# Two-layer decoder trunk on eight cores: the first value weights loaded in halves, token factors by bf16 rows, the last head slot undivided

## The chip, the cores and the metric

The kernel runs as one launch on the 8 cores of one Trainium2 chip. The metric is device time of the slowest core, in microseconds (us). Each core owns 1024 of the 8192 tokens and computes everything for them, with a halo of 2688 earlier tokens whose keys and values it works out again for itself. A core has TensorE (PE in the profile: matmuls, and PEld: its weight loads), VectorE (DVE), ScalarE (ACT), GpSimd (POOL) and SyncE (SP); here POOL and SP mostly issue DMA transfers.

## What is computed

Cut to the parts that matter here, the reference is:

```python
def _rms_norm(x, g):
    xf = x.astype(jnp.float32)
    y = xf * lax.rsqrt(jnp.mean(xf * xf, axis=-1, keepdims=True) + NORM_EPS)
    return (y * g.astype(jnp.float32)).astype(x.dtype)

def _dilated_attention_mixer(h, positions, w_in):     # layer 0
    q, k, v, q_mem = jnp.split(h @ w_in, [ATTN_W, 2 * ATTN_W, 3 * ATTN_W], axis=-1)
    q = _partial_rotary(q.reshape(b, s, ATTN_HEADS, HEAD_DIM), positions)
    k = _partial_rotary(k.reshape(b, s, ATTN_HEADS, HEAD_DIM), positions)
    ...
    for g, (window, dilation) in enumerate(((128, 1), (512, 4), (2048, 16))):
        o, l = _dilated_group(q[:, :, sl], k[:, :, sl], v[:, :, sl], window, dilation)
    ...                       # merged per head slot by the softmax denominators

for i in range(2):
    h = _rms_norm(x, mix_norm[i])
    mix_out, q_mem = mixer(h)   # layer 0: dilated attention, layer 1: spatial gating
    mem_out = _memory_attention(q_mem, _rms_norm(mem, mem_norm[i]), w_mem_kv[i])
    x = x + jnp.concatenate([mix_out, mem_out], axis=-1) @ w_out
    x = x + _swiglu(_rms_norm(x, ffn_norm[i]), w_gate[i], w_up[i], w_down[i])
return _rms_norm(x, final_norm)
```

D_MODEL is 2048, a head has 128 columns, and each of the three groups has four head slots.

## The kernel before

**Order.** All work on the five engines is recorded as operations with the regions they read and write. A list scheduler (`Prog.schedule`) then walks them by its own cost estimates and fixes the order on each engine; on the chip each engine runs its list strictly from front to back and waits by semaphores. So an operation that waits holds up everything behind it on its engine. A changed cost, cover or dependency can reorder the lists of all engines.

**The first stage.** It runs from 0 to about 345 us and makes the keys and values of the halo. The halo comes in blocks: 0 to 3 (512 tokens each, group with dilation 16), 4 (512, dilation 4) and 5 (128, dilation 1); the own tokens are two blocks of 512 (own 0, own 1, tile `hT`), and after them come the memory tokens. `norm_T` treats one block. Its `front` loads x transposed in four quarters of 0.5 MB on POOL's queue (into `stg_54` or `stg_55`, or `hT` for own blocks), squares each quarter on ACT (L592), adds two squares on DVE (L601), and sums over the features with four matmuls against ones (L603; block 0 skips the add, L597). The sum lies in PSUM bank 6 or 7, by turns from block to block. ACT turns it into the norm factor by Ln (L606) and Exp (L607), laid out along a row. For the raw blocks 0 to 4 the x tiles are only multiplied by the gain (L623, DVE); the norm factor is multiplied in later. The key path has it in its rotary tables (L693) and in L537. The value path needs it as a column per 128 tokens: four one-row fp32 matmuls (L610) turn the row into columns in the same bank, and DVE copies them out (L612). Own blocks are scaled on DVE at once (L621).

**The units.** `vunit` (L662) makes the values of 128 tokens with 16 matmuls of 512 columns into one of the banks 0 to 5, and ACT evicts them with the column factor (L671). `kunit` (L684) makes the keys of one head, 16 matmuls, and DVE applies the rotary (`rotary`: L537, L540, L541, L543, L545). `own_v` (L718) and `qk_units` (L766) do the same for own tokens. Weights come in 1 MB pieces into four ring slots (`Ring.load`, L455): two for the values of a group, two for its keys. In the listing here V0, K0, V1, K1 and so on are the units of block 0, 1 and so on. At the very start 24 matmuls on a constant (L811) run between the first sums.

**The attention.** `attend(s)` treats head slot s. Its last part (L1000 to L1009) takes the reciprocal of the softmax denominators (in banks 6 and 7) and multiplies the sums (banks 4 and 5) into `attnT`. For slots 0 to 2 that is one Ln (L1002) and one Exp (L1003) on ACT over 1024 columns and one multiply on DVE. For slot 3 it is divided in halves: Ln and Exp on ACT for the first 512 columns, a reciprocal on DVE (L1000) for the other 512, then two multiplies on DVE. After it the output projection begins (L1133).

Of the kernel before, what the change touches and what calls it, by code (L numbers as in the profile page):

```python
# [298 lines left out]
def build():  # L299
# [140 lines left out]
    class Ring:  # L440
# [5 lines left out]
        def load(self, src, half=False, at=None):  # L446
# [39 lines left out]
    one = small[112:113]  # L486
    dve(lambda v: v.memset(one, 1.0), [], [kreg("one")], 1)
# [64 lines left out]
    def norm_T(src_of, n, g0, keep_rs=None, own=None, raw=False):  # L552
# [22 lines left out]
        def front(after=(), pre=True):  # L575
            dmas = []
            for qd in range(4):
                dst = quarter(qd)
                if not pre and qd == 1:
# [69 lines left out]
    def halo_units(bi, nrm):  # L649
# [6 lines left out]
        def vunit(tt):  # L656
            def f():
                ws = [weights(("v", gi, h), w0[W0_V[gi][h]]) for h in range(2)]
                b = nextbank(P0B)
                for k0 in range(0, 16, 2):  # L660
# [1165 lines left out]
```

The softmax here doesn't subtract the row's maximum and nothing guards it: scores larger than these inputs give would overflow.

## Time and profile before

| | us |
|---|---|
| time, median of 3 runs | 2610.54 |
| lowest, highest run | 2609.48, 2611.22 |
| the profiled execution's own time | 2610.54 |
| its span on the slowest core, core 0 | 2608.9 |
| spans of the other cores | 2591.3 to 2606.8 |
| PE busy in the span | 2533.4 (97%) |
| DVE busy in the span | 1390.0 (53%) |
| ACT busy in the span | 712.7 (27%) |

Some 1.6 us of the time lie outside the span. All the rows below are of core 0. The start of a stage or a wait is in us from the span's start. A row of the timeline gives start, length, engine, line and operation, written tile and read tiles, and in brackets how long the engine had been idle before it and what ended that. Where the engine named had long been done, a DMA ended it.

### The profile page before, as it was taken

Reading aid. Unit: us, or ns where it says so; the run is one execution under the profiler, and the core shown is the slowest. Engines: PE = TensorE matmul, PEld = TensorE weight load, DVE = VectorE, ACT = ScalarE, POOL = GpSimd, SP = SyncE. Lnnn points to the kernel's source line nnn. Section 1 sums busy time; section 2 is a strip of 40 time slices with the busy share of each in tenths; the row PEclk is TensorE's granted clock in tenths of the full one; section 3 lists DMA queues with packets and bytes.
Section 4 is the critical chain, followed back from the end, with each engine's and each line's share of the span. In section 5 each row is a group of like instructions: output and inputs, shape, how many; then the busy total and the mean of one; then the engine's idle time right before and its main releaser. Section 6 shows DMA issues by size and latency. Waiting matters only on the chain.

```text
span 2608.9 us, 34534 instructions; the slowest of 8 cores (2591.3 to 2608.9 us)
## 1 busy us (share of the span) xinstructions
PE 2533.4 (97%) x12775; PEld 1191.2 (46%) x12775; DVE 1390.0 (53%) x2359; ACT 712.7 (27%) x1121; POOL 145.2 (6%) x247
## 2 busy tenths in 40 slices
PE   7999999999999999999999999999999999999997
PEld 3454445544444444444444444444444444444443
DVE  4862638867444443456667234237444444467666
ACT  3622134344222322210004431034222332210004
POOL 2100000000000000000000000000000000000002
PEclk9999999999999999999999999999999999999999
DMA  9845654345656656557644634334666656667554
GB/s 158 132 72 98 118 109 72 60 146 99 121 108 121 116 103 113 106 129 142 139 114 82 134 65 81 67 63 86 115 111 119 114 105 111 110 135 158 117 127 145
DMA packets 91893, 288.45 MB, mean 111 GB/s; under 512 B 6736, under 2 KB 56528, under 8 KB 68304
## 3 DMA queue, kind: packets, MB, share of 16 engines
q0 software_dynamic: 36912, 218.00, 48.7%
q1 hardware_dynamic: 54816, 68.24, 8.0%
q8 instruction: 104, 1.70, 0.3%
q14 instruction: 61, 0.50, 0.1%
HBM read 471.70 MB, written 32.51 MB: 193 GB/s over the span
## 4 chain that ended last, share of the span: by engine, by line
PE 89%; DMA 4%; DVE 4%; issue 2%; ACT 1%; POOL 0%; DVEq 0%; ACTq 0%; POOLq 0%; SPq 0%
PE psall L1243 39%; PE psall L1395 17%; PE psall L766 6%; PE psall L1634 4%; PE psall L1542 3%; PE psall L1591 3%; PE psall L684 3%; PE psall L662 2%; PE psall L718 2%; PE psall L1133 2%; DMA hid<-fs_74 1%; PE psall L1606 1%; PE psall L786 1%; PE psall L1098 1%; DMA stg_54<-xT 1%
## 5 line engine op out<-in xcount | busy, mean ns | idle before, releaser
L1034 DVE TENSOR_TENSOR xs<-psall,xs 128x512 f32<-128x512 f32 x400 | 270.2, 688 | 244.7 <-PE psall L1395 161.5
L1243 PE MATMUL psall<-hTq,ft_71 128*128 128x512 f16 x704 | 166.3, 379 | 0.6 <-DVE hTq L1123 0.6
L1243 PE MATMUL psall<-hTq,ft_72 128*128 128x512 f16 x704 | 166.3, 379 | 0.0
L1243 PEld LDWEIGHTS psall<-hTq,ft_71 128*128 128x128 f16 x704 | 68.7, 98 | 83.5 <-issue 0.9
L1243 PEld LDWEIGHTS psall<-hTq,ft_72 128*128 128x128 f16 x704 | 68.8, 98 | 82.6
L1243 PE MATMUL psall<-hTq,fr_67 128*128 128x512 f16 x384 | 87.3, 379 | 1.0 <-DVE hTq L1104 1.0
L1040 ACT ACTIVATE junkB_129<-xs 128x1024 bf16<-128x1024 f32 x16 | 16.8, 1052 | 248.2 <-DVE xs L1034 247.6
L1243 PE MATMUL psall<-Sq_65,ft_72 128*128 128x512 f16 (+2 forms) x368 | 83.5, 370 | 0.0
L1243 PE MATMUL psall<-Sq_65,ft_71 128*128 128x512 f16 (+2 forms) x368 | 83.5, 370 | 0.0
L1243 PE MATMUL psall<-Sq_64,ft_72 128*128 128x512 f16 x352 | 83.2, 379 | 0.0
L1243 PE MATMUL psall<-Sq_64,ft_71 128*128 128x512 f16 x352 | 83.2, 379 | 0.0
L1243 PE MATMUL psall<-hTq,fr_70 128*128 128x512 f16 x352 | 79.9, 379 | 0.0
L1243 PE MATMUL psall<-hTq,fr_69 128*128 128x512 f16 x352 | 79.7, 379 | 0.0
L1243 PE MATMUL psall<-hTq,fr_68 128*128 128x512 f16 x320 | 72.7, 379 | 0.0
L1040 ACT ACTIVATE junkB_128<-xs 128x1024 bf16<-128x1024 f32 x8 | 8.5, 1057 | 233.3 <-DVE xs L1034 232.8
L1222 DVE TENSOR_TENSOR ft_71<-fr_67 128x2048 f16<-128x2048 f16 x22 | 26.9, 1225 | 82.5 <-PE psall L1243 81.8
L1222 DVE TENSOR_TENSOR ft_72<-fr_70 128x2048 f16<-128x2048 f16 x20 | 24.5, 1225 | 84.8 <-PE psall L1243 84.8
L1222 DVE TENSOR_TENSOR ft_71<-fr_69 128x2048 f16<-128x2048 f16 x20 | 24.5, 1225 | 83.1 <-PE psall L1243 83.1
L1222 DVE TENSOR_TENSOR ft_72<-fr_68 128x2048 f16<-128x2048 f16 x20 | 24.5, 1224 | 80.0 <-PE psall L1243 79.4
L1104 DVE TENSOR_TENSOR hTq<-psall,gT_s 128x1024 f16<-128x1024 f16 x48 | 56.9, 1218 | 17.7 <-PE psall L1098 17.2
L1249 ACT COPY snap_79<-psall 128x512 f32<-128x512 f32 x59 | 34.5, 585 | 113.5 <-PE psall L1243 113.5
L1249 ACT COPY snap_77<-psall 128x512 f32<-128x512 f32 x58 | 34.0, 585 | 115.1 <-PE psall L1243 115.1
(1341 smaller groups left out, 4726.4 us busy)
## 6 DMA issues: line engine op xcount, KB each, us to landing
fr_67<-wgu POOLq DMA_DIRECT2D x24, 1024.0 KB, 9.5
fr_69<-wgu POOLq DMA_DIRECT2D x22, 1024.0 KB, 9.8
fr_70<-wgu POOLq DMA_DIRECT2D x22, 1024.0 KB, 9.1
fr_68<-wgu POOLq DMA_DIRECT2D x20, 1024.0 KB, 9.5
ring_0_137<-w POOLq DMA_DIRECT2D x8, 1024.0 KB, 9.2
xs<-xo SPq DMA_DIRECT2D x8, 1024.0 KB, 10.2
y<-xs SPq DMA_DIRECT2D x16, 512.0 KB, 4.1
ring_0_138<-w POOLq DMA_DIRECT2D x7, 1024.0 KB, 10.5
```

The lines of the kernel that those rows point to most:

```text
L662: pe([(lambda t, k=k, w=w: t.matmul(bank(b), hb[k * n + tt * 128:k * n + tt * 128 + 128], w[(k % 8) * 512:(k % 8 + 1) * 512], start=(k == ...
L684: pe([(lambda t, k=k: t.matmul(bank(b)[:, 0:n], w[k * 256 + c0:k * 256 + c0 + 128], hb[k * n:(k + 1) * n], start=(k == 0), stop=(k == 15)) ...
L766: proj(b, 512, [(lambda t, k=k: t.matmul(bank(b), w[k * 256 + c * 128:k * 256 + c * 128 + 128], hT[k * TOK + th * 512:k * TOK + th * 512 + ...
L1034: dve(lambda v: v.tensor_tensor(out=xa, in0=bank(b), in1=xa, op=ALU.add), [PB(b), xr], [xr], 512)
L1104: dve(lambda v, b=b, gb=gb, dst=dst: v.tensor_tensor(out=dst, in0=bankb(b).rearrange("p (a c) -> p a c", c=128), in1=gb, op=ALU.mult), [PB ...
L1222: dve(lambda v: v.tensor_tensor(out=T[0:2048], in0=w[1024:3072], in1=w[0:2048], op=ALU.subtract), [w.r(0, 3072)], [T.r(0, 2048)], 2048, 2)
L1243: pe([(lambda t, k=k: t.matmul(bank(b)[:, lo:lo + n], W[blk * 1024 + k * 128:blk * 1024 + k * 128 + 128], f(k)[:, lo:lo + n], start=(first ...
L1249: act(lambda a: a.copy(out=s_.ap, in_=bank(b)), [PB(b)], [s_.r()], 512)
L1395: pe([(lambda t, k=k: t.matmul(bank(b), f(u, k), w[k * 512:(k + 1) * 512], start=(first and k == 0), stop=(last and k == hG - 1), skip_gro ...
L1542: pe([(lambda t_, k=k, b=b, hf=hf, ws=ws, t=t: t_.matmul(bank(b), hTq[hq_(hf * 8 + k, t * 128, 128)], ws[hf][k * 512:(k + 1) * 512], start ...
L1591: proj(b, 512, [(lambda t, k=k, b=b, c=c, th=th, w=w: t.matmul(bank(b), w[k * 256 + c * 128:k * 256 + c * 128 + 128], hTq[hq_(k, th * 512, ...
L1634: pe([(lambda t_, k=k, hh=hh, hf=hf: t_.matmul(bank(b), gTm[(hh * 8 + k) * TOK + t * 128:(hh * 8 + k) * TOK + t * 128 + 128], ws[hh][k * 5 ...
```

## The change

Four things change, all in the first stage and in the last head slot.

1. **Halves.** The two 1 MB pieces of the first value weights are loaded in halves of 0.5 MB. On POOL's queue each half stands behind one quarter of block 0's x. A value matmul waits for the half that it reads, no longer for the whole piece. The load of the position table (`tki`) waits for the first half in place of the constants. 16 matmuls on a constant remain of 24.
2. **Token factors.** ACT casts the row of norm factors to bf16 (hi), DVE subtracts it from the fp32 row (lo, bf16), and eight bf16 matmuls of one column each, hi and lo for four token tiles, sum both into columns. They are recorded not in `front` but by the block's second value unit, and the evictions of the first two value units are recorded behind them.
3. **Banks.** Keys of block 5 and the memory units of layer 0 take banks 0 to 5 in place of 2 to 5.
4. **Last head slot.** It is treated as slots 0 to 2 are, undivided.

```diff
+    rhl = [sb(f"rhl{i}", 196 * KB + 1024 * i, 1024) for i in range(2)]
...
+                for i in range(2):
+                    sl = slice(i * 2048, (i + 1) * 2048)
+                    parts.append(lambda sl=sl, i=i: pooldma(lambda g: g.dma_start(out=rb[sl], in_=src[:, sl]), [], [rb.r(sl.start, sl.stop)],
+                                                            f"w{at}{'b' * i}", 1.05))
...
                 dmas.append(pooldma(lambda g, dst=dst, qd=qd: g.dma_start(out=dst, in_=src_of(qd)), [],
                                     qreg(qd), f"x{sid}_{qd}", 4 * n * 512 / 1e6, after=after))
+                if between is not None:
+                    between[qd]()
...
+            def cols():
+                col = small[104 + 4 * sid:104 + 4 * sid + n // 128]
+                hi, lo = rhl
+                act(lambda a: a.copy(out=hi[0:n][0:1], in_=rb[0:n][0:1]), [rb.r(0, n)], [hi.r(0, n)], n)
+                dve(lambda v: v.tensor_tensor(out=lo[0:n][0:1], in0=rb[0:n][0:1], in1=hi[0:n][0:1], op=ALU.subtract),
+                    [rb.r(0, n), hi.r(0, n)], [lo.r(0, n)], n, lat=3)
+                pe([(lambda t, tt=tt, i=i: t.matmul(bank(b)[:, tt:tt + 1], rhl[i][tt * 128:(tt + 1) * 128][0:1], ones[0:1, 0:1],
+                                                    start=(i == 0), stop=(i == 1)))
+                    for tt in range(n // 128) for i in range(2)], [hi.r(0, n), lo.r(0, n), ON_R], [PB(b)], 1)
+                dve(lambda v: v.tensor_copy(out=col, in_=bank(b)[:, 0:n // 128]), [PB(b)], [kreg(f"col{sid}")], 4)
             if raw:
-                col = small[104 + 4 * sid:104 + 4 * sid + n // 128]
-                pe([(lambda t, tt=tt: t.matmul(bank(b)[:, tt:tt + 1], rb[tt * 128:(tt + 1) * 128][0:1], one[0:1], start=True, stop=True))
-                    for tt in range(n // 128)], [rb.r(0, n), kreg("one")], [PB(b)], 128)
-                dve(lambda v: v.tensor_copy(out=col, in_=bank(b)[:, 0:n // 128]), [PB(b)], [kreg(f"col{sid}")], 4)
+                cols_.append(cols)
...
-                       [w.r()] + [hb.r(k * n + tt * 128, k * n + tt * 128 + 128) for k in (k0, k0 + 1)], [PB(b)], 512)
+                       [w.r(k0 % 8 * 512, (k0 % 8 + 2) * 512)] + [hb.r(k * n + tt * 128, k * n + tt * 128 + 128) for k in (k0, k0 + 1)], [PB(b)], 512)
...
-                    act(lambda a: a.activation(out=dst, in_=src, func=AF.Copy, scale=rs), [PB(b), kreg(f"col{sid}")],
-                        Vh.r3(4, HALO, tile * 128, tile * 128 + 128), 512)
+                    nrm[4].append(lambda: act(lambda a: a.activation(out=dst, in_=src, func=AF.Copy, scale=rs), [PB(b), kreg(f"col{sid}")],
+                                              Vh.r3(4, HALO, tile * 128, tile * 128 + 128), 512))
+                    if tt:
+                        for f in nrm[4]:
+                            f()
+                        nrm[4].clear()
                     return
...
-                b = nextbank(P0B if raw else (2, 3, 4, 5))
+                b = nextbank(P0B)
...
+        act(lambda a: a.activation(out=rden.ap, in_=denA, func=AF.Ln), [PB(6), PB(7)], [rden.r()], 1024, tbl="exp")
+        act(lambda a: a.activation(out=rden.ap, in_=rden.ap, func=AF.Exp, scale=-1.0), [rden.r()], [rden.r()], 1024, tbl="exp")
...
-            if h == 1:
-                dve(lambda v, rd=rd: v.reciprocal(rd, bank(7)), db, [rr], n)
...
+        dve(lambda v: v.tensor_tensor(out=row.rearrange("p (m r) -> p m r", r=16), in0=by_tok(accA), in1=by_tok(rden.ap), op=ALU.mult),
+            [PB(4), PB(5), rden.r()], [attnT.r(s * TOK, (s + 1) * TOK)], 1024)
```

The new lines shift the numbers in the changed kernel: the sums are L607 and L613, the value units L680, the key units L706, the columns L625, the constant matmuls L835, the squares L602, Ln and Exp L616 and L617.

TensorE, from the end of block 0's sums, before: sums of x (L597) with matmuls on a constant (L811), the columns (L610), then V0 from ring slots 137 and 138 and K0 from 139.

```order
L811 MATMUL psall<-cmat_s 128x512 x5
L597 MATMUL psall<-sq_51,cmat_s 128x512 x4
L811 MATMUL psall<-cmat_s 128x512 x2
L610 MATMUL psall<-small,rsr_125 128x1 x4
L662 MATMUL psall<-ring_0_137,stg_54 128x512 x32
L662 MATMUL psall<-ring_0_138,stg_54 128x512 x32
L684 MATMUL psall<-stg_54,ring_0_139 128x512 x32
```

TensorE, from its first operation, after: V0 (L680) reads ring slots 139 and 140, which now name the first value weights; `stg_54` is block 0's x.

```order
L680 MATMUL psall<-ring_0_139,stg_54 128x512 x4
L607 MATMUL psall<-sq_51,cmat_s 128x512 x4
L680 MATMUL psall<-ring_0_139,stg_54 128x512 x12
L835 MATMUL psall<-cmat_s 128x512 x4
L607 MATMUL psall<-sq_52,cmat_s 128x512 x4
L835 MATMUL psall<-cmat_s 128x512
L680 MATMUL psall<-ring_0_139,stg_54 128x512 x16
L835 MATMUL psall<-cmat_s 128x512 x4
L607 MATMUL psall<-sq_53,cmat_s 128x512 x4
L835 MATMUL psall<-cmat_s 128x512
L680 MATMUL psall<-ring_0_140,stg_54 128x512 x16
L835 MATMUL psall<-cmat_s 128x512 x4
```

V0 has moved in between the sums of block 0, a quarter's worth at a time.

TensorE around own 0's first sum, before: L603 on `sq_52` is the second sum of block 2, L603 on `sq_51` the first sum of own 0; L684 is K1 and L662 with `stg_54` V2.

```order
L603 MATMUL psall<-sq_52,cmat_s 128x512 x4
L684 MATMUL psall<-stg_55,ring_0_139 128x512 x8
L684 MATMUL psall<-stg_55,ring_0_140 128x512 x8
L610 MATMUL psall<-small,rsr_125 128x1 x4
L684 MATMUL psall<-stg_55,ring_0_140 128x512 x8
L662 MATMUL psall<-ring_0_137,stg_54 128x512 x2
L603 MATMUL psall<-sq_51,cmat_s 128x512 x4
L684 MATMUL psall<-stg_55,ring_0_140 128x512 x8
L662 MATMUL psall<-ring_0_137,stg_54 128x512 x12
L662 MATMUL psall<-ring_0_138,stg_54 128x512 x2
L603 MATMUL psall<-sq_53,cmat_s 128x512 x4
```

The same place after: the first L613 is the second sum of block 2, the next the first sum of own 0; then come tiles of V2 (L680).

```order
L613 MATMUL psall<-sq_52,cmat_s 128x512 x4
L613 MATMUL psall<-sq_51,cmat_s 128x512 x4
L680 MATMUL psall<-ring_0_139,stg_54 128x512 x8
L680 MATMUL psall<-ring_0_140,stg_54 128x512 x8
L680 MATMUL psall<-ring_0_139,stg_54 128x512 x6
L613 MATMUL psall<-sq_53,cmat_s 128x512 x4
L680 MATMUL psall<-ring_0_139,stg_54 128x512 x2
L680 MATMUL psall<-ring_0_140,stg_54 128x512 x2
```

Own 0's first sum now follows block 2's second sum directly, and 32 matmuls of V2 stand ahead of the second half of K1 (`ring_0_142`), which stood ahead of nearly all of V2.

ScalarE at the same place, after: L602 on `hT` are the squares of own 0, L616 and L617 are Ln and Exp, on `rsr_125` for block 2 and on `rsb_123` for own 0.

```order
L602 ACTIVATE sq_51<-hT 128x2048
L616 ACTIVATE rsr_125<-psall,small 128x512
L602 ACTIVATE sq_52<-hT 128x2048
L617 ACTIVATE rsr_125<-rsr_125 128x512
L602 ACTIVATE sq_53<-hT 128x2048
L602 ACTIVATE sq_51<-hT 128x2048
L616 ACTIVATE rsb_123<-psall,small 128x512
L617 ACTIVATE rsb_123<-rsb_123 128x512
L622 CAST rhl_127<-rsr_125 1x512
L689 ACTIVATE Vh<-psall,small 128x4x128 x4
```

Block 2's Ln stands between own 0's first and second square, and the evictions of V1 (L689) stand behind own 0's Exp and block 2's cast.

ScalarE around block 3's norm, after: L602 on `stg_55` are its squares, L602 on `hT` those of own 1, `rsr_126` is block 3's factor.

```order
L602 ACTIVATE sq_51<-stg_55 128x2048
L602 ACTIVATE sq_52<-stg_55 128x2048
L602 ACTIVATE sq_53<-hT 128x2048
L616 ACTIVATE rsr_126<-psall,small 128x512
L617 ACTIVATE rsr_126<-rsr_126 128x512
L602 ACTIVATE sq_51<-hT 128x2048
L689 ACTIVATE Vh<-psall,small 128x4x128 x3
L602 ACTIVATE sq_52<-hT 128x2048
L689 ACTIVATE Vh<-psall,small 128x4x128
L622 CAST rhl_127<-rsr_126 1x512
```

ScalarE at that place, before, where the same Ln and Exp are L606 and L607.

```order
L592 ACTIVATE sq_51<-stg_55 128x2048
L671 ACTIVATE Vh<-psall,small 128x4x128 x2
L592 ACTIVATE sq_53<-hT 128x2048
L592 ACTIVATE sq_52<-stg_55 128x2048
L592 ACTIVATE sq_52<-hT 128x2048
L606 ACTIVATE rsr_126<-psall,small 128x512
L592 ACTIVATE sq_51<-hT 128x2048
L607 ACTIVATE rsr_126<-rsr_126 128x512
L592 ACTIVATE sq_53<-hT 128x2048
```

In both, squares of own 1 stand ahead of block 3's Ln; on TensorE the columns of block 2 (L625), which share bank 6 with block 3's sum, now stand behind that Ln:

```order
L706 MATMUL psall<-stg_54,ring_0_141 128x512 x24
L613 MATMUL psall<-sq_52,cmat_s 128x512 x4
L706 MATMUL psall<-stg_54,ring_0_141 128x512 x8
L613 MATMUL psall<-sq_51,cmat_s 128x512 x4
L625 MATMUL psall<-cmat_s,rhl_127 128x1
L625 MATMUL psall<-cmat_s,rhl_128 128x1
```

Before, block 2's columns (L610 in the fence of TensorE above) were made ahead of V2.

## Rows read from the trace of the kernel before

**Rows 1.** The page's list of busy time: TensorE, weight loads and the other engines.

```profile
PE 2533.4 (97%) x12775; PEld 1191.2 (46%) x12775; DVE 1390.0 (53%) x2359; ACT 712.7 (27%) x1121; POOL 145.2 (6%) x247
```

**Rows 2.** Timeline of the opening on TensorE: columns, V0's second half, K0, V1.

```profile
28.12 1.02 PE L610 MATMUL psall<-small,rsr_125 1*128 1x1 f32 x8 [1.32 <-ACT rsr_125 L607]
...
37.73 7.07 PE L662 MATMUL psall<-ring_0_138,stg_54 128*128 128x512 bf16 x32
...
44.64 7.07 PE L684 MATMUL psall<-stg_54,ring_0_139 128*128 128x512 bf16 x32
...
58.45 2.75 PE L662 MATMUL psall<-ring_0_137,stg_55 128*128 128x512 bf16 x12
```

**Rows 3.** Timeline of POOL's queue: when two ring pieces are issued.

```profile
5.39 0.59 POOL L455 DMA_DIRECT2D ring_0_138<-w  x1
5.91 0.60 POOL L455 DMA_DIRECT2D ring_0_139<-w  x1
```

**Rows 4.** DMA issues, 0 to 110 us: times, size of one, us to landing.

```profile
ring_0_138<-w POOLq DMA_DIRECT2D x1, 1024.0 KB, 29.9
ring_0_139<-w POOLq DMA_DIRECT2D x1, 1024.0 KB, 35.4
```

**Rows 5.** Timeline, 58 to 94 us: an add, a square, an Ln, K1's end.

```profile
58.44 1.20 DVE L601 TENSOR_TENSOR sq_52<-sq_52,sq_53 128x2048 bf16<-128x2048 bf16 x1
...
82.18 1.91 ACT L592 ACTIVATE sq_51<-hT 128x2048 bf16<-128x2048 bf16 x1
...
83.98 0.69 ACT L606 ACTIVATE rsr_125<-psall,small 128x512 f32<-128x512 f32 x1
...
91.27 1.89 PE L684 MATMUL psall<-stg_55,ring_0_140 128*128 128x512 bf16 x8
```

**Rows 6.** Timeline of POOL's queue: loads of block 3 (second pair), then own 1.

```profile
93.70 1.07 POOL L582 DMA_DIRECT2D stg_55<-xT  x2 [1.92 <-PE psall L684]
94.74 3.01 POOL L582 DMA_DIRECT2D hT<-xT  x4
```

**Rows 7.** DMA issues near 94 us: size of one, us to landing.

```profile
stg_55<-xT POOLq DMA_DIRECT2D x2, 512.0 KB, 12.7
...
hT<-xT POOLq DMA_DIRECT2D x1, 512.0 KB, 16.8
```

**Rows 8.** Waits of TensorE, 95 to 600 us: us in total, times, longest.

```profile
PE psall L1133 <- DVE attnT L1009: 5.8, 1, 5.8
...
PE psall L718 <- DVE hT L621: 1.6, 1, 1.6
PE psall L603 <- DVE sq_52 L601: 1.5, 1, 1.5
```

**Rows 9.** Stretches: length, busy us by engine, granted clock (PEclk), DMA share, GB/s.

```profile
198.00:199.00 1.00, 1.00 (x6) 0.55 (x5) 0.02 (x1) 0.88 (x2) 0.00 (x0) 1.00 1.02 213
...
300.00:301.00 1.00, 1.00 (x4) 0.30 (x2) 0.00 (x0) 0.00 (x0) 0.00 (x0) 0.50 0.95 164
...
545.00:554.00 9.00, 5.25 (x13) 1.61 (x14) 5.34 (x7) 1.87 (x4) 0.00 (x0) 0.50 0.70 210
```

**Rows 10.** Timeline: a ring slot's load, and the matmul that waited for it.

```profile
287.57 0.53 POOL L455 DMA_DIRECT2D ring_0_138<-w  x1 [8.11 <-PE psall L662]
...
297.78 0.59 PE L766 MATMUL psall<-hT,ring_0_138 128*128 128x512 bf16 x2 [3.72 <-DVE t_1_118 L540]
```

**Rows 11.** Timeline of the end of slot 0 (undivided), then of slot 3 (halves).

```profile
415.98 1.03 ACT L1002 ACTIVATE rden_121<-psall 128x1024 f32<-128x1024 f32 x1
...
418.28 1.89 DVE L1009 TENSOR_TENSOR attnT<-psall,rden_121 128x1024 bf16<-128x1024 f32 x1
...
542.84 0.60 ACT L1002 ACTIVATE rden_121<-psall 128x512 f32<-128x512 f32 x1 [3.10 <-PE psall L951]
...
548.59 0.58 PE L1133 MATMUL psall<-ring_0_139,attnT 128*128 128x512 bf16 x1 [5.85 <-DVE attnT L1009]
```

**Rows 12.** Instructions of one line, 402 to 404 us: ns, min/median/max.

```profile
L928 PE MATMUL psall<-QK_47,KTh x9: 193/193/219, 402.2 to 403.1; 128*128 128x64 bf16 x8, 128*128 128x128 bf16 x1
```

More of the change, by code:

```diff
@@ L444, in build, with load @@
         gen = {}
-        def load(self, src, half=False, at=None):
+        def load(self, src, half=False, at=None, parts=None):
             if at is None:
@@ L485, in build @@
     dve(lambda v: v.memset(eps_ap, EPS), [], [kreg("eps")], 1)
-    one = small[112:113]
-    dve(lambda v: v.memset(one, 1.0), [], [kreg("one")], 1)
     act(lambda a: a.activation(out=small[254:255], in_=eps_ap, func=AF.Ln), [kreg("eps")], [kreg("warm")], 1, tbl="exp")
@@ L573, in qreg, with front @@
             return [sg.r(k * step + base, k * step + base + n) for k in range(qd * 4, qd * 4 + 4)]
-        def front(after=(), pre=True):
+        cols_ = []
+        def front(after=(), pre=True, between=None):
             dmas = []
@@ L629, in scale @@
             return f
-        return front, [scale(k) for k in range(16)], sg, (rb, sid)
+        return front, [scale(k) for k in range(16)], sg, (rb, sid), cols_
     def x_src(bi):
@@ L732, in f @@
                 w = weights(("mk", layer, m // 2), wkv[layer * 4 + m // 2])
-                b = nextbank((0, 1) if layer else (2, 3, 4, 5))
+                b = nextbank((0, 1) if layer else P0B)
                 c0 = (m % 2) * 128
@@ L744, in f @@
                 ws = [weights(("mv", layer, h), wkv[layer * 4 + 2 + h]) for h in range(2)]
-                b = nextbank((0, 1) if layer else (2, 3, 4, 5))
+                b = nextbank((0, 1) if layer else P0B)
                 for hf in range(2):
@@ L800, in build @@
     n0 = xnorm(0)
-    n0[0](pre=False)
-    weights(("v", 2, 0), w0[W0_V[2][0]])
-    weights(("v", 2, 1), w0[W0_V[2][1]])
-    spdma(lambda q: q.dma_start(out=tki.ap, in_=posr), [kreg("cm")], [tki.r()], "c5", 0.5)
+    v0p = []
+    for h in range(2):
+        rb = R.load(w0[W0_V[2][h]], parts=v0p)
+        held["v", 2, h] = (rb, R.gen[rb.off // KB])
+    n0[0](pre=False, between=v0p)
+    spdma(lambda q: q.dma_start(out=tki.ap, in_=posr), [held["v", 2, 0][0].r(0, 2048)], [tki.r()], "c5", 0.5)
     for h in range(2):
@@ L811, in build @@
     warm = [P.op("pe", lambda t: t.matmul(bank(WB).rearrange("p (a b) -> p a b", b=128), ones, M_own.unsqueeze(1).to_broadcast([128, 4, 128]), start=True, stop=True), [ON_R, OW_R], [], 0.43, prio=1e9)
-            for _ in range(24)]
+            for _ in range(16)]
     n1 = xnorm(1)
@@ L991, in attend @@
         state["prev"]()
+        act(lambda a: a.activation(out=rden.ap, in_=denA, func=AF.Ln), [PB(6), PB(7)], [rden.r()], 1024, tbl="exp")
+        act(lambda a: a.activation(out=rden.ap, in_=rden.ap, func=AF.Exp, scale=-1.0), [rden.r()], [rden.r()], 1024, tbl="exp")
         row = attnT[s * TOK:(s + 1) * TOK]
-        for h in range(2) if s == 3 else (None,):
-            sl, hs = (slice(0, TOK), slice(0, 16)) if h is None else (slice(h * 512, h * 512 + 512), slice(h * 8, h * 8 + 8))
-            n, nr = sl.stop - sl.start, hs.stop - hs.start
-            rd, rr = rden[sl], rden.r(sl.start, sl.stop)
-            ab, db = ([PB(4), PB(5)], [PB(6), PB(7)]) if h is None else ([PB(4 + h)], [PB(6 + h)])
-            if h == 1:
-                dve(lambda v, rd=rd: v.reciprocal(rd, bank(7)), db, [rr], n)
-            else:
-                act(lambda a, rd=rd, sl=sl: a.activation(out=rd, in_=denA[:, sl], func=AF.Ln), db, [rr], n, tbl="exp")
-                act(lambda a, rd=rd: a.activation(out=rd, in_=rd, func=AF.Exp, scale=-1.0), [rr], [rr], n, tbl="exp")
-        for h in (1, 0) if s == 3 else (None,):
-            sl, hs = (slice(0, TOK), slice(0, 16)) if h is None else (slice(h * 512, h * 512 + 512), slice(h * 8, h * 8 + 8))
-            n, nr = sl.stop - sl.start, hs.stop - hs.start
-            by_tok = lambda a, nr=nr: a.rearrange("p (r m) -> p m r", r=nr)
-            out = row.rearrange("p (m r) -> p m r", r=16)[:, :, hs]
-            dve(lambda v, out=out, sl=sl, by_tok=by_tok: v.tensor_tensor(out=out, in0=by_tok(accA[:, sl]), in1=by_tok(rden[sl]), op=ALU.mult),
-                ([PB(4), PB(5)] if h is None else [PB(4 + h)]) + [rden.r(sl.start, sl.stop)], [attnT.r(s * TOK, (s + 1) * TOK)], n)
+        by_tok = lambda a: a.rearrange("p (r m) -> p m r", r=16)
+        dve(lambda v: v.tensor_tensor(out=row.rearrange("p (m r) -> p m r", r=16), in0=by_tok(accA), in1=by_tok(rden.ap), op=ALU.mult),
+            [PB(4), PB(5), rden.r()], [attnT.r(s * TOK, (s + 1) * TOK)], 1024)
     def x_load(t, after=()):
```

4 lines of the change are left out of this document (3 added, 1 removed).

## The prediction

> **What bounds the kernel now.** I read the busy times first. TensorE works 97% of the span and no other engine is above 53% [rows 1]; so time is won only where TensorE waits, runs at its lower clock, or does work that can go. All edits lie in the first stage (to 345 us) and at the end of head slot 3 (543 us), and from there the program is the same; a microsecond won or lost is passed on to the end. I then read where TensorE waits there: the opening until K0 starts at 44.64 [rows 2], one wait of 1.6 and two of 1.5 (the second of them not shown), one of 5.8 at slot 3's end [rows 8], and one of 3.72 [rows 10]. The granted clock came third: behind the 1.5 us wait at 197.5 it stays at 1.00 (2.4 GHz), behind those of 3.7 and 5.8 us it is 0.50 (1.2 GHz) for a while [rows 9]. At the upper level matmuls of 512 columns lie (44.64 - 37.73) / 32 = 0.216 us apart [rows 2]. The sum is made against the profiled execution, 2610.54 us, 1.6 of it outside the span; it is also the median.
>
> **The opening.** Before, V0 begins after the last x quarter's norm and ends at 44.64; after, V0 follows the x quarters and the weight halves. The total up to the second weight piece is unchanged, so its last half lands where that piece did: 5.39 + 29.9 = 35.3 [rows 3, 4]. Behind it are 16 matmuls, 3.5 us, and the columns: TensorE is through at 39. But K0 needs the next piece, which lands at 5.91 + 35.4 = 41.3, in the same place of the queue as before. So K0 starts at 41.4 in place of 44.64: **-3.2**. That is the cap of this edit, not V0's 15 us. The eight constant matmuls that go stood in waits for DMA and are worth nothing.
>
> **The columns.** Before, four fp32 matmuls are eight passes, 1.02 us [rows 2], five times (one row stands for them). After, eight one-column bf16 matmuls. The nearest row has nine small bf16 ones start between 402.2 and 403.1, with other work among them [rows 12]: eight take 0.8 at most and nothing at least; I take 0.27, because other matmuls filled most of that stretch. That saves 0.75 each time, between 0.2 and 1.0: **-3.75** in all, where nobody waits for them. The cast and the subtraction (a row of 512, priced like an Ln, 0.69 [rows 5]) lie beside TensorE's work.
>
> **First new wait: own 0's first sum.** K0 takes 58.45 - 44.64 = 13.8 [rows 2] and ends at 55.2; 112 matmuls, sums among them, reach to the end of block 2's second sum, 112 x 0.216 = 24.2: 79.4. Before, 26 matmuls and the columns, 6.6 us, stood between that sum and own 0's first one. After, the two follow directly, and the order of ScalarE puts block 2's Ln ahead of own 0's second square. So the chain from sum to sum lies open: Ln 0.69, square 1.91, add 1.20 [rows 5], 0.2 for hand-overs: **+4.0**, within 0.3 either way, to 83.4. It hangs on no transfer, and an earlier or later arrival does not change it. Queued behind the waiting sum on TensorE stand V2's tiles.
>
> **Small waits up to K1's end.** Own 0's second sum waits for its last quarter's square and add (0.6), block 1's columns for own 0's Ln, which shares bank 7 (0.2), K1's second half for V1's evictions, which now stand behind Exp and cast (0.5): **+1.3**, from nothing to 2.5.
>
> **Second new wait: block 3's norm.** K1's second half now stands behind 32 matmuls of V2. Before, K1 ends at 91.27 + 1.89 = 93.2 [rows 5]. After: 83.4 + own 0's two sums 1.7 + 32 of V2 6.9 + the small waits 1.3 + 32 of K1 6.9 = 100.2, 7 us later (6.4 at the reads that POOL waits for). POOL's loads of block 3 and own 1 wait for K1's reads of `stg_55` [rows 6], and move by 6.4. Before, block 3's last quarter lands at about 94.2 + 12.7 = 107 and own 1's first at 94.74 + 16.8 = 111.5 [rows 6, 7]; after, at 113.4 and 118. TensorE arrives at block 3's second sum behind 64 more matmuls and a sum, 14.7, at 114.9; square and add [rows 5] are done at 116.6 (1.7 lost). Block 2's columns behind it share bank 6 with that sum and wait for its Ln, and ScalarE holds that Ln behind own 1's first square, which ends at 118 + 1.9 = 119.9: the columns come at 120.6 (3.0 lost). V3's first matmuls then wait for the first K2 head's rotary (2.2, its chain on DVE), and 0.5 is spread: **+7.4**. Bounds: 3 if the transfers land 4 us sooner in a quiet queue, 9 if DVE is behind. The 1.6 us wait before own 0's values [rows 8] is then covered: **-1.6**.
>
> **Clock.** Work at 0.50 costs half its busy time: 5.25 us of it behind the 5.85 us wait, 2.6 [rows 9]; behind the 3.72 us wait some 3.3 us ran at it (one of them shown), 1.6. The new waits are 4.0 and, with little work between, 1.7 + 3.0 + 2.2. I take 1.6 and 2.1: **+3.7**; nothing to 5.2. The Trainium skill (TensorE: Matmul & The Clock Gate, HAM oscillation — how this bites in real kernels) advises finishing a product's K tiles before waiting for DMA, lest the clock fall in each wait. That speaks against V0 by quarters. The trace agrees for a wait of 3.72, not for one of 1.5 [rows 9].
>
> **A ring slot later.** Block 5's values free a slot for query weights, which came 297.7 - 287.57 = 10.1 us after their issue, 3.72 of them waited for [rows 10]. In the new order that read stands one query piece of eight matmuls later against what covers the load: **+1.7**, from nothing to 2.7 if the clock falls further.
>
> **Last head slot.** Before, 548.59 - 542.84 = 5.75 [rows 11]. Undivided as in slot 0, from Ln's start to the multiply's end: 418.28 + 1.89 - 415.98 = 4.2, and a hand-over of 0.1 [rows 11]. **-1.5**. The wait is still longer than 3.72, so its slow stretch stays. Banks 0 to 5 for block 5's keys and the memory, and the dropped memset, cost nothing: their units lie behind queries that TensorE has ready.
>
> **Sum.** -3.2 - 3.75 + 4.0 + 1.3 + 7.4 - 1.6 + 3.7 + 1.7 - 1.5 = +8.05: 2610.5 + 8.0 = **2618.5**. With the low terms (no small waits, second wait 3, no clock, no slot) it is -3.1, 2607.4; with the high ones (2.5, 9, 5.2, 2.7) +13.4, 2623.9.
>
> **Rivals.**
>
> *The opening at half clock.* V0 now runs in bursts between landings; if the level is 0.50 there, the 16 matmuls behind the last half take 16 x 0.43 = 6.9, the columns are through at 42.5, the gain falls to 2.0, and K0's first eight matmuls pay 1.7: 2618.5 + 1.2 + 1.7 = 2621.4. This is what that section of the Trainium skill (TensorE: Matmul & The Clock Gate) would make of it. For it: behind the wait of 3.72 us it fell to 0.50 [rows 9]. Against it: at 198 us, behind a wait of 1.5, it is 1.00 [rows 9], and the bursts leave waits of about that length: a megabyte lands in 41.3 - 35.3 = 6 us, and 25 matmuls of a quarter fill 5.4 of them. That the halves don't do what they say (the last quarter's square or scale holds V0 up) ends at the same time. Chance 0.15.
>
> *The lag is absorbed* (not slower). Downstream lie waits of 1.5, 1.5 and 3.72 [rows 8, 10]. If what ends them does not move with TensorE, because it hangs on transfers issued early, they swallow up to 5 of the lag: 2613.5; if the clock also holds through the broken second wait, 2611.4. It decides once these waits shrink to under 0.5. Against it: those loads are issued when TensorE frees a buffer, as the one of 287.57 was. Chance 0.28.
>
> *The loads win* (faster). If block 3's and own 1's transfers land 5 us sooner, the second wait is at most 2, the small waits go and the clock holds: -3.2 - 3.75 + 4.0 + 2.0 - 1.6 - 1.5 = -4.05; with one wait of 1.5 downstream covered 2605, and with columns that save 1.0 each 2603.7. For it: only eight transfers stand in that queue. Against it: so it was before, and the last took 12.7 and 16.8 [rows 7]. Chance 0.17.
>
> **How the numbers follow.** Forecast 0.40, half clock 0.15, absorbed 0.28, loads win 0.17. About 0.2% (5.2 us) is what a measurement of this kernel tells from no change. So slower 0.55, same 0.28, faster 0.17. The range takes in the absorbed case, most of the faster one (2603) and the high bound with the half clock's 1.2 on it: 2603 to 2626. The likeliest case alone spans 2615 to 2625.
>
> **What would show it.** Right: K0 at 41 to 42; TensorE idle for about 4 us before own 0's first sum near 80 us; block 3's POOL issues at 96 to 101; three waits between 114 and 124; a granted clock of 0.50 behind them; the last slot's wait at 4.3. Wrong: a sum of own 0 that follows block 2's without a gap, K1 ending before 95, or a clock of 1.00 from 80 to 130 us.

## The result: slower, by the two waits and what they drag along

| | before | after |
|---|---|---|
| time, median of 4 runs, us | 2610.88 | 2625.22 |
| ratio to before, 95% interval | | 1.0051 [1.0031, 1.0070] |
| profiled execution's own time | 2610.54 | 2621.14 |
| its span on the slowest core | 2608.9 (core 0) | 2619.5 (core 2) |
| TensorE busy in the span | 2533.4 | 2527.6 |

The changed kernel is slower by 0.51%, some 13 us, though TensorE is busy 6 us less. The ratios here and below leave out executions in which some cores were disturbed; without the one such execution of the changed kernel (2902 us) its median is 2624.2. The profiled execution is the shortest of the changed kernel's, 10.6 us above that of before, and the readings below explain that one.

Waits of TensorE from 30 to 600 us, after (us in total, times, longest). They answer to [rows 8].

```profile
PE psall L613 <- DVE sq_51 L611: 7.8, 2, 4.1
PE psall L788 <- DMA ring_0_140<-w: 5.5, 1, 5.5
PE psall L1144 <- DVE attnT L1020: 4.8, 1, 4.8
PE psall L613 <- DVE sq_53 L611: 3.0, 1, 3.0
PE psall L680 <- DVE t_0_119 L547: 2.9, 2, 2.6
PE psall L706 <- DMA ring_0_141<-w: 1.7, 1, 1.7
PE psall L613 <- DVE sq_52 L611: 1.7, 2, 1.1
PE psall L625 <- ACT rsr_126 L616: 1.2, 1, 1.2
```

The wait of 1.6 before own values is gone. New are two waits for squares of a norm (7.8 in two), one for columns (1.2) and one for a rotary (2.6); longer are those for the query weights (5.5, before 3.7) and for the memory's norm (3.0, before 1.5). In the timeline of TensorE the new ones stand here:

```profile
41.15 6.85 PE L706 MATMUL psall<-stg_54,ring_0_141 128*128 128x512 bf16 x31 [1.74 <-DMA ring_0_141<-w]
...
78.94 1.02 PE L613 MATMUL psall<-sq_52,cmat_s 128*128 128x512 bf16 x4
84.01 1.17 PE L613 MATMUL psall<-sq_51,cmat_s 128*128 128x512 bf16 x4 [4.05 <-DVE sq_51 L611]
...
95.31 7.07 PE L706 MATMUL psall<-stg_55,ring_0_142 128*128 128x512 bf16 x31
...
120.80 1.02 PE L613 MATMUL psall<-sq_51,cmat_s 128*128 128x512 bf16 x4 [3.75 <-DVE sq_51 L611]
123.01 0.16 PE L625 MATMUL psall<-cmat_s,rhl_127 1*128 1x1 bf16 x1 [1.19 <-ACT rsr_126 L616]
...
125.95 1.01 PE L680 MATMUL psall<-ring_0_139,stg_55 128*128 128x512 bf16 x2 [2.59 <-DVE t_0_119 L547]
```

K0 starts at 41.15, before at 44.64 [rows 2]. The sum at 78.94 is block 2's second, that at 84.01 own 0's first. ScalarE shows what lies between them: block 2's Ln, then own 0's second square.

```profile
80.06 0.69 ACT L616 ACTIVATE rsr_125<-psall,small 128x512 f32<-128x512 f32 x1 [0.79 <-PE psall L613]
80.64 1.90 ACT L602 ACTIVATE sq_52<-hT 128x2048 bf16<-128x2048 bf16 x1
...
117.41 1.91 ACT L602 ACTIVATE sq_52<-stg_55 128x2048 bf16<-128x2048 bf16 x1 [1.50 <-DMA stg_55<-xT]
120.38 1.91 ACT L602 ACTIVATE sq_53<-hT 128x2048 bf16<-128x2048 bf16 x1 [1.06 <-DMA hT<-xT]
122.20 0.67 ACT L616 ACTIVATE rsr_126<-psall,small 128x512 f32<-128x512 f32 x1
```

The second group belongs to the waits near 120. The 3.75 us of the sum at 120.80 are a wait for block 3's last quarter: its square starts at 117.41, when its transfer has landed. Own 1's first square, which also waited for its transfer, stands ahead of block 3's Ln; that adds only some 0.4 us to the 1.19 of the columns, since the sum ends at 121.82 and the Ln starts at 122.20. POOL issued block 3's loads at 90.69 and 93.70 [rows 6] before, at 99.47 and 102.91 after:

```profile
90.69 1.09 POOL L582 DMA_DIRECT2D stg_55<-xT  x2 [27.33 <-PE psall L684]
```

```profile
99.47 1.08 POOL L590 DMA_DIRECT2D stg_55<-xT  x2 [39.93 <-PE psall L706]
102.91 1.05 POOL L590 DMA_DIRECT2D stg_55<-xT  x2 [2.36 <-PE psall L706]
```

Granted clock, after (columns as in [rows 9]): in the opening, behind the two waits, behind the memory's norm, and at the last head slot.

```profile
15.00:30.00 15.00, 14.77 (x58) 5.97 (x57) 2.28 (x8) 3.82 (x2) 0.00 (x0) 1.00 1.04 188
...
86.00:88.00 2.00, 2.00 (x7) 0.63 (x5) 1.97 (x5) 1.44 (x1) 0.00 (x0) 0.50 0.00 1
...
126.00:128.00 2.00, 2.00 (x5) 0.64 (x6) 1.94 (x3) 2.00 (x4) 0.00 (x0) 0.50 1.16 193
...
267.00:269.00 2.00, 2.00 (x6) 0.65 (x5) 0.00 (x0) 0.58 (x1) 0.00 (x0) 0.50 0.57 119
...
560.00:565.00 5.00, 5.00 (x18) 1.96 (x17) 2.10 (x4) 1.87 (x4) 0.00 (x0) 0.74 0.92 272
```

Behind the waits of 4.05, of 7.5 in three and of 2.96 us the level is 1.2 GHz for a while; the row of 267 is new, behind the memory's wait. That wait, before and after:

```profile
256.64 0.60 PE L603 MATMUL psall<-sq_53,cmat_s 128*128 128x256 bf16 x4 [1.51 <-DVE sq_53 L601]
```

```profile
264.34 0.60 PE L613 MATMUL psall<-sq_53,cmat_s 128*128 128x256 bf16 x4 [2.96 <-DVE sq_53 L611]
```

It is not the same on every core: on the other seven of the changed kernel's profiled execution it is between 0 and 1.7 us.

How far the changed kernel lies behind, at the same operation in both:

| operation | before | after | behind |
|---|---|---|---|
| K0 starts | 44.64 | 41.15 | -3.5 |
| own values start | 141.17 | 149.09 | 7.9 |
| first sum of the memory's norm | 256.64 | 264.34 | 7.7 |
| queries behind the ring load | 297.78 | 310.67 | 12.9 |
| output projection starts | 548.59 | 559.74 | 11.2 |
| end of the span | 2608.9 | 2619.5 | 10.6 |

All of it is lost before 311 us, and a little given back at the last head slot. The 7.7 of the memory's row is too small by 1.7: in the changed kernel one piece of eight matmuls of own values stands behind that sum which stood ahead of it before.

### The profile page after: what moved, and what is told of

It is laid out like the page before. It is cut to its first block, busy times and chain, and to the rows that moved or that the text cites. A ratio compares the mean times of both kernels' runs of the same rounds, so it can differ in the third digit from the quotient of the medians.

```text
span 2619.5 us, 34458 instructions; the slowest of 8 cores (2601.2 to 2619.5 us)
## 1 busy us (share of the span) xinstructions
PE 2527.6 (96%) x12688; PEld 1188.4 (45%) x12767; DVE 1388.7 (53%) x2361; ACT 717.1 (27%) x1126; POOL 146.1 (6%) x249
## 4 chain that ended last, share of the span: by engine, by line
PE 87%; DMA 6%; DVE 4%; issue 3%; ACT 1%; POOL 0%; DVEq 0%; ACTq 0%; POOLq 0%; SPq 0%
PE psall L1254 39%; PE psall L1406 18%; PE psall L788 6%; PE psall L1645 4%; PE psall L1602 3%; PE psall L740 2%; PE psall L1553 2%; DMA stg_55<-xT 2%; PE psall L1144 2%; PE psall L680 2%; PE psall L706 1%; PE psall L808 1%; DMA ring_0_215<-wkv 1%; DMA hid<-fs_74 1%; PE psall L1109 1%
```

## The experiments

Two theories stood at first. D: recording the columns late (the deferral) costs. H: the halves cost, because V0's early start reorders everything behind it.

**e1: the deferral undone.**

```diff
-                cols_.append(cols)
+                cols()
...
-                    nrm[4].append(lambda: act(lambda a: a.activation(out=dst, in_=src, func=AF.Copy, scale=rs), [PB(b), kreg(f"col{sid}")],
-                                              Vh.r3(4, HALO, tile * 128, tile * 128 + 128), 512))
-                    if tt:
...
+                    act(lambda a: a.activation(out=dst, in_=src, func=AF.Copy, scale=rs), [PB(b), kreg(f"col{sid}")],
+                        Vh.r3(4, HALO, tile * 128, tile * 128 + 128), 512)
```

> The changed kernel with one thing undone: the columns of token factors are recorded in the block's own norm again (still cast, subtract and eight bf16 matmuls), and each value eviction right behind its unit. Theory D (the deferral costs): recorded by the second value unit, a block's columns stand behind the next norm that uses the same PSUM bank, and so the value evictions, their banks and the second half of K1 wait for that norm. Without it the 4.1 us wait before own 0's first sum and the three waits between 116 and 126 us (7.5) go, the loads of block 3 are issued at 88 to 94 us, and the time falls by 8 to 13 us from the changed kernel, to 2610 to 2616. Theory H (the halves cost, because V0's early start reorders everything): the waits near 80 and 120 stay within 2 us of what they are, time 2620 or more. If all the opening's gain is kept as well, 2604 or less.

Ratio to before 1.0017 [0.9994, 1.0039]: no measurable difference from before. It lies under the changed kernel's 1.0051, though the ends of the two intervals overlap (1.0039 and 1.0031); of the nine executions that its ratio takes in, eight took 2607.9 to 2616.1 us and one 2634.1, the changed kernel's three 2621.1 to 2626.2. Its waits of TensorE, 30 to 600 us:

```profile
PE psall L736 <- DVE hT L639: 6.7, 1, 6.7
PE psall L1140 <- DVE attnT L1016: 4.4, 1, 4.4
PE psall L613 <- DVE sq L611: 3.2, 2, 1.8
PE psall L784 <- DVE t L549: 3.2, 1, 3.2
```

None of the waits near 80 and 120 us is left; block 3's loads are issued at 86.1 and 90.4. But one wait of 6.7 stands before own values, where before it was 1.6 [rows 8]: what the opening won is spent there. On the eight cores this wait is 4.55 to 6.97 us, before 1.60 on each. It is one for VectorE's scalings, and on the slowest core these in turn wait 1.40 for ScalarE's Exp of own 1, ahead of which ScalarE's order has two squares of block 4, one of them held up by its transfer:

```profile
132.64 1.91 ACT L602 ACTIVATE sq<-stg 128x2048 bf16<-128x2048 bf16 x1 [3.26 <-DMA stg<-xT]
...
136.83 0.62 ACT L617 ACTIVATE rsb<-rsb 128x512 f32<-128x512 f32 x1
```

```profile
137.55 8.04 DVE L639 SCALAR_TENSOR_TENSOR hT<-hT,gT_s,rsb 128x512 bf16<-128x512 bf16 x12 [1.40 <-ACT rsb L617]
```

On the core with the 4.55 VectorE has no idle time ahead of the scalings. So by these rows VectorE's list makes most of this wait, and ScalarE's order with block 4's transfer the rest.

**e2: the deferral alone, on the kernel before**, with its fp32 columns.

```diff
-            if raw:
+            def cols():
                 col = small[104 + 4 * sid:104 + 4 * sid + n // 128]
...
+            if raw:
+                cols_.append(cols)
...
+                    nrm[4].append(lambda: act(lambda a: a.activation(out=dst, in_=src, func=AF.Copy, scale=rs), [PB(b), kreg(f"col{sid}")],
```

> The kernel before with one thing done: its four fp32 column matmuls are recorded by the block's second value unit, behind the first two units, and their evictions behind them. Loads, banks, last slot as before. Theory D: 2619 to 2626, with waits of 6 to 9 us in all at block 3's norm near 115 to 125 us and block 3's loads issued 6 to 11 us later than before. Theory H: within 3 us of before (2608 to 2614), no wait over 2 us between 75 and 140.

1.0074 [1.0058, 1.0090], some 19 us: more than the whole change, and above the range that D gave. In its timeline of TensorE the waits near 120 and at the query weights are back:

```profile
122.45 1.02 PE L605 MATMUL psall<-sq,cmat_s 128*128 128x512 bf16 x4 [3.42 <-DVE sq L603]
124.78 1.83 PE L612 MATMUL psall<-small,rsr 1*128 1x1 f32 x8 [1.31 <-ACT rsr L608]
129.19 1.01 PE L666 MATMUL psall<-ring,stg 128*128 128x512 bf16 x2 [2.58 <-DVE t L541]
...
312.77 9.81 PE L774 MATMUL psall<-hT,ring 128*128 128x512 bf16 x32 [5.38 <-DMA ring<-w]
```

POOL issues block 3's loads at 101.5 and 104.9. Own 0's first sum does not wait here: in its place stand smaller waits, 2.08 for a rotary at 83.26, 0.93 for columns at 93.39, and 1.19 for V1's evictions at 95.60. D holds from both sides: with the deferral taken out the waits go, with it alone waits come, near 80 us in another form. The parts do not add up, though: e2, e3 and e4 alone come to 1.0094, the whole change to 1.0051. One reason can be seen in e3, whose wait before own values the changed kernel does not have, since its TensorE arrives there late. The 5.4 us wait for the query weights comes with it too; e1 has it at 3.2.

**e3: the halves alone, on the kernel before**, with the finer waits of the value matmuls and 16 constant matmuls.

```diff
+    v0p = []
+    for h in range(2):
+        rb = R.load(w0[W0_V[2][h]], parts=v0p)
...
+    n0[0](pre=False, between=v0p)
```

> The kernel before with the first value weights in halves between the x quarters, the finer waits of the value matmuls, 16 constant matmuls and the position table behind the first half; columns, banks and last slot as before. K0 starts at 41.2 in place of 44.6. Theory D: no wait of 4 us at own 0; but the opening's 3.4 us don't reach the end, because VectorE's list before own values (rotary of K2, then 16 scalings of hT) is worked off without a gap and ends at the same time or later: the wait before own values grows from 1.6 to 4 to 6 us, time 2608 to 2615. Theory H: 2618 or more. If TensorE were the bound there, 2607.

1.0026 [1.0014, 1.0037], 4 to 10 us slower, about 2617: a little under what H says, a little over what D says, and more than a lost gain. K0 starts at 41.47, and the wait before own values is 4.3:

```profile
143.34 11.06 PE L727 MATMUL psall<-ring,hT 128*128 128x512 bf16 x40 [4.28 <-DVE hT L630]
```

Busy time of VectorE (third pair) in two stretches, of before and of e3:

```profile
15.00:30.00 15.00, 9.62 (x44) 4.11 (x42) 4.16 (x14) 7.04 (x5) 0.00 (x0) 0.97 1.04 191
60.00:83.00 23.00, 23.00 (x111) 10.82 (x110) 16.72 (x41) 14.37 (x12) 3.36 (x5) 1.00 1.09 166
```

```profile
15.00:30.00 15.00, 14.24 (x58) 5.83 (x57) 2.28 (x8) 3.82 (x2) 0.00 (x0) 1.00 1.04 185
60.00:83.00 23.00, 23.00 (x111) 10.83 (x110) 21.30 (x50) 16.50 (x14) 0.87 (x2) 1.00 1.09 172
```

With the halves VectorE is busy for only 2.3 of 15 us in the opening and is full from 60 to 83 (21.3 of 23): the rotary tables, which were made while V0 ran, now come later and push the rotaries and scalings that own values wait for.

**e4: the last head slot alone, on the kernel before.** The edit is the diff's part on that slot.

> The kernel before with only the last head slot undivided. The wait before the output projection falls from 5.85 to 4.3 to 4.8 us (the changed kernel shows 4.76), the half-level stretch behind it stays: 1.0 to 1.6 us less, 2609 to 2610. Rival: the wait is short enough for the clock to stay up for most of it, 2 us more: 2606 to 2608.

0.9994 [0.9982, 1.0007]. The wait before the output projection is 4.8, before 5.8 [rows 8], and the clock is 0.50 behind it as it was, for some 4.4 us of work in place of 5.9. A microsecond of waiting and less than one of clock, under what can be measured; the clock rival came at most in part.

**e5: e1 with the position table loaded at once.**

```diff
-    spdma(lambda q: q.dma_start(out=tki.ap, in_=posr), [held["v", 2, 0][0].r(0, 2048)], [tki.r()], "c5", 0.5)
+    spdma(lambda q: q.dma_start(out=tki.ap, in_=posr), [], [tki.r()], "c5", 0.5)
```

> The kernel of e1 with the load of the position table issued at once, without a wait. Theory V (VectorE's list is what holds own values): in e1 VectorE idles in the opening (2.3 us busy of 15 to 30) and makes the rotary tables until 52 us, where before they were done at 47; the delay is handed on through the rotaries and the 16 scalings to own values, which wait 6.7 us. With the table earlier VectorE is done with the tables by 40, its busy time of 60 to 83 us falls from 21.3 to 17 to 19, and the wait before own values falls to 2.5 to 4.5 us; time 2 to 5 us less than e1, 2607 to 2611. Rival (the wait is set by the landing of own 1, which this does not move): the wait stays at 6 to 7, time as e1.

0.9991 [0.9981, 1.0002], against e1's 1.0017: some 7 us less by the estimates, though the intervals overlap. VectorE, from the stretches of e5:

```profile
15.00:30.00 15.00, 13.35 (x53) 5.35 (x53) 12.34 (x21) 6.16 (x4) 0.00 (x0) 1.00 1.04 164
60.00:83.00 23.00, 23.00 (x115) 10.44 (x113) 20.57 (x48) 15.95 (x14) 3.45 (x5) 1.00 1.07 166
```

The tables are made in the opening now (12.3 busy), and the wait before own values is 4.3 in place of 6.7, as expected. But 60 to 83 falls to 20.6 only, not to 17 to 19: one reading is that the earlier K0 brings other work of VectorE forward into that stretch; it was not tested. Nor is VectorE's list all of what is left: the scalings still wait 0.79 for ScalarE's Exp on the slowest core. The expectation was right on the wait and wrong on that number.

**e6: two piece sizes, on the kernel before.** The first own values go in pieces of 2 matmuls, block 5's in pieces of 8.

```diff
-                for hf in range(2):
+                st_ = 2 if gi == 2 else 8
+                for k0 in range(0, 16, st_):
...
-                for k0 in range(0, 16, 2):
+                kp = 8 if bi == 5 else 2
+                for k0 in range(0, 16, kp):
```

> The kernel before with two changes of piece size and nothing else: the first own values are recorded in pieces of 2 matmuls in place of 8, so that a piece waits for two scalings and not for eight; block 5's values in pieces of 8 in place of 2, so that query pieces no longer come between them and their ring slot is free some 7 us earlier. The waits of 1.6 (own values) and 3.7 us (query weights) go, and the half-level stretch behind the second: 1.6 + 3.2 + 1.6 less, 2603 to 2606. Rival (planner's order shifts waits elsewhere): within 2 us of before.

0.9984 [0.9972, 0.9997], about 4 us faster; the 6.4 that were expected lie within the interval (0.8 to 7.3). Its waits, 30 to 600 us:

```profile
PE psall L1135 <- DVE attnT L1011: 5.9, 1, 5.9
PE psall L603 <- DVE sq L601: 4.8, 2, 2.7
PE psall L737 <- DMA ring<-wkv: 1.3, 1, 1.3
```

The waits of 1.6 and 3.7 are gone. Part of the gain is given back to block 5's and the memory's sums (4.8 in two, before 1.5 each), and the clock falls behind both, to 0.69 in the mean of 195 to 200 us.

**e7: e5 with the piece sizes of e6.**

> The kernel of e5 with the two changes of piece size of e6. If the opening's 3.4 us were held up only by the wait before own values, they reach the end here: 2599 to 2604, faster than e6 by 1 to 4. If VectorE's list is the limit, TensorE waits in small steps among the own values, and the time is that of e6 or up to 3 more.

0.9974 [0.9961, 0.9987]: about 7 us faster than before and 20 us faster than the changed kernel by the two ratios. It is the best of all by the estimates, but its interval overlaps those of e6 and e8. The waits in small steps that were expected among the own values did not come; after half a microsecond they run on:

```profile
139.58 10.68 PE L738 MATMUL psall<-ring,hT 128*128 128x512 bf16 x48 [0.51 <-DVE hT L639]
```

They start at 139.58, before at 141.17, but these are two different cores. K0 on the same core of e7:

```profile
43.12 5.30 PE L703 MATMUL psall<-stg,ring 128*128 128x512 bf16 x16 [2.00 <-DMA ring<-w]
```

That is 1.5 ahead of before's 44.64, and own values are 1.6 ahead. As the mean of the eight cores, K0 starts 1.9 us earlier in e7 than in e6 (41.35 and 43.21) and own values 2.1 (136.0 and 138.1): what the opening wins gets through to own values here.

**e8: the halves with fp32 columns and the divided slot, the table at once, the piece sizes.**

> The kernel of e3 (halves alone, fp32 columns, divided slot) with the position table issued at once and the two changes of piece size. It differs from e7 by the columns and the last slot: 0 to 3 us from e7, either way, 2600 to 2605.

0.9985 [0.9971, 1.0000]. The interval overlaps that of e7, and e8 differs from e7 in the banks of change 3 as well, so that what the bf16 columns, the undivided slot and the banks give together is between nothing and a few us; not settled. Neither the bf16 columns nor the banks were run alone.

**e9: the changed kernel with its columns in another bank.** Why does the deferral cost? One reading is the bank: block 1's columns, recorded behind own 0's norm, share bank 7 with it and must follow its Ln.

```diff
+                cb = nextbank((0, 1, 2, 3, 4, 5))
...
-                pe([(lambda t, tt=tt, i=i: t.matmul(bank(b)[:, tt:tt + 1], rhl[i][tt * 128:(tt + 1) * 128][0:1], ones[0:1, 0:1],
+                pe([(lambda t, tt=tt, i=i: t.matmul(bank(cb)[:, tt:tt + 1], rhl[i][tt * 128:(tt + 1) * 128][0:1], ones[0:1, 0:1],
```

> The changed kernel with one thing changed: the columns of token factors go to a bank of 0 to 5 and no longer to the norm's own bank 6 or 7; they are still recorded by the second value unit. Theory B (of the deferral it is the shared bank that costs): no wait over 1.5 us before own 0's first sum, K1 done by 92, no waits of 7 us between 105 and 126, time as e1, 2608 to 2614. Rival O (the place in the record costs too, since it sets which operation goes first on each engine): the wait before own 0 goes, but waits of 5 to 9 us in all remain near block 3's norm and own 1's (105 to 125 us); 2616 to 2626.

It has no ratio: its profiled execution took 2625.5 us, one of before on the same chip 2616.2, 9 us less. Its waits, 30 to 600 us:

```profile
PE psall L613 <- DVE sq L611: 6.6, 4, 1.9
PE psall L789 <- DMA ring<-w: 6.0, 1, 6.0
PE psall L1145 <- DVE attnT L1021: 4.4, 1, 4.4
PE psall L613 <- DVE small L629: 4.1, 1, 4.1
```

The wait before own 0's first sum shrinks to 1.6, and block 3's loads are issued at 93.1 and 95.3. But 6.4 us of waits remain near block 3's norm and own 1's (1.7, 0.6 and 4.1). So in this execution another bank takes away 2.4 of the first wait's 4.05 us and 6.3 of the 8.8 us by which block 3's loads were late. The bank alone does not bring that wait, since e2 has the shared bank and none at that sum. Waits near 120 us stay with the late place in the record, though in another form (the 4.1 is own 1's first sum), and e1, which differs in that place, has none: the waits speak for rival O, the time of one execution settles nothing. Which operation of ScalarE or VectorE is out of turn there was not tried one by one.

## Why the prediction was right, and where its terms were off

Forecast 2618.5, range 2603 to 2626, slower with 0.55; measured 2625.2, slower. Point by point, in the order of its parts:

- **Opening**: -3.2 forecast, -3.5 measured (K0 at 41.15). The landing of K0's weights is the cap, as said: TensorE waits 1.7 for it. Luck has a share in so close a match: in one execution K0 starts at 40.97 to 46.94 on the eight cores before and at 38.95 to 41.78 after. The means are 43.7 and 40.3, 3.4 apart.
- **Columns**: 0.75 saved each time forecast. The starts of the eight span only 0.19 us, but the four fp32 ones must be measured in the same way, from the columns' start to the start of what follows: 93.50 to 93.76 after, 0.26, and 160.29 to 161.27 before, 0.98. That saves 0.72. But the sum took it five times, and only four count: block 0's columns lie ahead of K0's wait for its weights, which the opening's term had already priced. So -2.9 in place of -3.75.
- **First new wait**: +4.0 forecast, 4.05 measured, with Ln, square and add in the order named. It was the surest step, because it was read from the order on ScalarE and TensorE together and, as said, hung on no transfer: it is 4.05 to 4.10 on all eight cores, though own 0's quarters land at different times on them.
- **Small waits**: +1.3 forecast up to K1's end, 0.3 measured; 0.66 before block 1's first sum, at 57.30, was not forecast. Together 1.0.
- **Second new wait**: +7.4 forecast, 3.75 + 1.19 + 2.59 = 7.5 measured. The sum held, the parts did not: 1.7, 3.0 and 2.2 were forecast. That the sum held is luck. On the eight cores the three come to some 5.3 on four and 6.75 to 7.7 on the others, and the columns' 3.0 came on no core (0.9 to 1.7); a late transfer of block 3's last quarter made it up. Block 3's loads came 9 us later than before and not 6.4, since the first wait's fall of the clock (level 0.50 at 86 to 88) also held up K1, on whose reads they wait: the term for the clock and the term for the loads were added as if independent. The -1.6 before own values came as forecast.
- **Clock**: 3.7 forecast for the two waits. Some 3.2 us of work ran at the half level behind the first and 3.1 behind the second, half of which is lost: 3.2 together.
- **Ring slot**: +1.7 forecast, 5.50 - 3.72 = 1.8 measured. e2 shows that the deferral brings the longer wait (5.38; e1 has 3.2); in e6, with pieces of 8, there is none.
- **Last slot**: -1.5 forecast for the wait, 5.85 - 4.76 = -1.1 measured. The rows of 560 to 565 us at 0.74 mean some 2.6 us of half-level work, before 5.25 and more [rows 9]; so about 1.3 more came back than forecast, in this execution. e4 shows about half of that second part.
- **Missing term**: the memory's norm. Its wait grew from 1.51 to 2.96, and the clock fell behind it (0.50 at 267 to 269; before it did not): 1.5 + 1.7. The sum left the waits for sums downstream as they were, and the prediction had looked at them only as possible relief in the rival of the absorbed lag. They did the reverse, at least on the slowest core; on the other seven this wait is 1.7 at most.

With what was measured the sum is -3.5 - 2.9 + 4.05 + 1.0 + 7.5 - 1.6 + 3.2 + 1.8 - 2.4 + 3.2 = +10.4 of the 10.6 of the profiled execution, against +8.0 forecast. So the mechanism was right in its main steps; the columns were taken once too often, the memory's norm was left out, and the slowest core's transfers happened to fit the second wait. Why other executions of the changed kernel took 3 to 5 us more than the profiled one stays open.

The rivals. *Opening at half clock* did not come: V0's bursts ran at 1.00 from 15 to 30 us, with 14.8 of 15 us busy. The Trainium skill (TensorE: Matmul & The Clock Gate, HAM oscillation — how this bites in real kernels) warns of waiting for DMA between K tiles; in this trace the waits between the bursts were under 1 us, so its case did not arise here. *Absorbed* did not come: the wait that was to shrink under 0.5, for the query weights, grew from 3.72 to 5.50. *The loads win* did not come: block 3's loads were issued 9 us later. Where they come early, in e1 at 86 and 90 us, there is no second wait, but e1 differs in its order too, and e9, with loads at 93 and 95, still has 6.4 us of waits; so early loads alone are not shown to be enough. e1 also shows what the prediction did not see at all: even then the opening's gain does not reach the end, because own values wait for VectorE's scalings, and these for its list and for ScalarE's Exp. The -3.2 was carried to the end in every case of the sum; in e1 6.7 us of waiting on the slowest core, 4.55 to 6.97 on the eight, stand against it. In the changed kernel that did not show, since TensorE was late by more.

## What to carry to other kernels

In a kernel whose order is fixed by a list, an operation's place in the record is a cost of its own: moving four tiny matmuls, and the evictions that wait for them, behind the next user of their bank cost more (e2, 19 us) than the whole opening had to give. Ahead of shortening a stretch of the bounding engine, ask which other engine's list ends at the next meeting point; here VectorE's did, with ScalarE's order behind it. With VectorE's tables moved forward and TensorE starting on two scalings in place of eight (e7), the opening's gain reached own values, though in time e7 is not clear of e6. And where rows show the clock fall behind a wait, price the wait with that fall, and the fall with what it delays (here K1, and with it the next block's loads).

## What the runs showed that was not expected

- A wait of 2.96 us was followed by the half level (0.50 at 267 to 269 us), one of 1.5 at the same place before was not; in e6 one of 2.7 was (0.69 in the mean of 195 to 200 us). The prediction went by the waits of 1.5, 3.7 and 5.85. Before, the level also fell in the opening (row below): behind waits of 1.89, 1.90 and 1.32 us, the last shorter than the 1.5 that left it at 1.00. So the length of the last wait alone does not tell what the level does behind it.
- Eight one-column bf16 matmuls, in four pairs that each add into one column, start some 0.03 us apart (39.07 to 39.26 us, after), though each stands for 0.16 us in the trace.

TensorE in the opening, before, behind those three waits:

```profile
30.00:31.00 1.00, 1.00 (x4) 0.36 (x3) 0.89 (x3) 0.00 (x0) 0.00 (x0) 0.50 1.19 188
```
